# First transfers in pieces on two queues, first weights rounded in halves, two jobs' products in another order, half the warming products

## The chip, the cores and the metric

The kernel runs on one core of a Trainium2 chip. The metric is the device time of one execution in microseconds (us). Three runs of the kernel before took 1553.55, 1553.56 and 1553.8 us, so the median is 1553.56 us. The engines are called by their names in the profile: PE (TensorE, with PEld for its weight loads), DVE (VectorE), ACT (ScalarE), POOL (GpSimd) and SP (SyncE, which only issues transfers here).

## The reference, cut to what matters

Two transformer-like blocks run one behind the other on 512 tokens with 1024 features. The first has a gated recurrence, sparse attention chosen by an indexer, and a feed-forward part; the second has linear attention, window attention, cross attention and a convolutional feed-forward part. The change touches only the first microseconds, where the input is normed and the first columns of the first projection are made:

```python
def hybrid_layer(x, norm1_w, w_in, ...):
    h = rms_norm(x, norm1_w)
    u = h @ w_in
    rnn_x, rnn_gate, q, k, v, iq, ik, iw, g = jnp.split(u, offsets, axis=-1)
    ik = rms_norm(ik, idx_k_norm_w)
    y_attn = dsa_attention(q, k, v, iq, ik, iw)
    ...
```

All operands are fp32.

## The kernel before

**Jobs.** Activations lie with features on the 128 partitions and tokens along the row: `x` is 8 tiles of 128x512. A job makes 128 output features: its weights are one slot of `w_raw`, 128x1024, which are 8 blocks of 128x128, one for each input tile. There are four slots. Every factor is cut into a high part (rounded to fp32r) and a rest: ACT writes `w_hi` from `w_raw`, POOL writes `w_lo = w_raw - w_hi` in four pieces of 128x256, ACT writes `a_hi = x * norm1`, and DVE writes `a_lo`, the rest of that product. PE adds three products for each of the 8 tiles: `w_hi a_hi`, `w_hi a_lo` and `w_lo a_hi`, thus 24 products of 128x512 a job. The division by the root mean square of a token is made later, on the job's output, so that the jobs can start before the norm is known.

**The start.** Job 0 (J_IK: the indexer's keys and weights) and job 1 (J_IQ, the first tile of its queries) are written out by hand, product by product, so that PE can use whatever is ready: `whole` issues `w_hi a_hi`, `input_rest` issues `w_hi a_lo`, `weight_rest` issues `w_lo a_hi`. Everything is issued in order on each engine and waits on semaphores: `xhi_ready` counts the tiles of `a_hi`, `xlo_ready` those of `a_lo`, `hi_ready` the finished slots of `w_hi`, `lo_ready` the pieces of `w_lo`. Ahead of them PE multiplies zeros (the warming products, L696) since its clock starts low. From job 2 on `job` issues the three products of a tile in turn (L634 to L636).

**Transfers.** SP's queue is q1 in the profile, ACT's is q10. Before the change ACT issues `vec` (all 326 columns of the norms' and biases' values, 163 KB), four transfers of two tiles of `x` each (512 KB), and `cst` (276 KB). SP issues the weights of job 0 at once, and those of jobs 1 to 3 (512 KB each) each behind the landing of the next transfer of `x`. Weights from job 4 on wait for POOL to free their slot.

**Squares.** Behind `a_hi`, ACT squares the tiles of `x` and DVE adds them into `acc`; PE sums `acc` over the partitions behind job 2 (`norm_sum`), ACT takes the root, DVE the inverse, and PE spreads it within job 3.

Of the kernel before, what the change touches and what calls it, by code (L numbers as in the profile page):

```python
# [29 lines left out]
ACT = mybir.ActivationFunctionType  # L30
# [3 lines left out]
P = 128  # L34
T = 512
# [5 lines left out]
SLOTS = 4  # L41
# [3 lines left out]
J_IK = 0  # L45
J_IQ = 1
# [131 lines left out]
NVEC = 0  # L178
# [48 lines left out]
def build(nc, w_all, x_t, mem_t, vecs, consts, rg_w, consts2, row_table, out):  # L227
    with ExitStack() as ctx:
# [7 lines left out]
        raw = sb("w_raw", [P, SLOTS, KT * P])  # L236
        w_hi = sb("w_hi", [P, SLOTS, KT * P], F32R)
# [5 lines left out]
        vec = sb("vec", [P, NVEC])  # L243
        cst = sb("cst", [P, 4 * P + 40])
# [194 lines left out]

        @block.sync  # L440
        def _(sp):
            for sl in range(SLOTS):
                if sl >= 1:
                    sp.wait_ge(x_landed[sl], 16)
                sp.dma_start(raw[:, sl], w_all[sl]).then_inc(raw_landed[sl], 16)
            with sp.Fori(1, J_IN2 // SLOTS) as i:
                for sl in range(SLOTS):
# [176 lines left out]
        def _(pe):  # L624
# [67 lines left out]
                block_of(k, range(5, 8), hi, lo, width, 7, early(k, 0)).then_inc(s("job_done"), 1)  # L692

            pe.wait_ge(s("zeros_ready"), 1)
            for _ in range(5):
                mm(o_ps[:], p1[:, 0, 0:P], p1[:, 0, :], start=True, stop=True)  # L696

            def whole(k, kts):

                for kt in kts:  # L700
                    if k == J_IK:
                        pe.wait_ge(s("xhi_ready"), kt + 1)
                    if kt == 0:
# [24 lines left out]
            weight_rest(J_IK, (0, 1))
            whole(J_IK, (2, 3))
            weight_rest(J_IK, (2, 3))  # L730
            input_rest(J_IK, (1,))
            whole(J_IK, (4, 5))
            weight_rest(J_IK, (4, 5))
            input_rest(J_IK, (2,))
            whole(J_IK, (6, 7))
            weight_rest(J_IK, (6, 7))
            input_rest(J_IK, (3, 4))
            whole(J_IQ, (0, 1))
            input_rest(J_IK, (5,))
            whole(J_IQ, (2, 3, 4))  # L740
            weight_rest(J_IQ, (0, 1))
            input_rest(J_IK, (6,))
            whole(J_IQ, (5, 6, 7))
            weight_rest(J_IQ, (2, 3))
            input_rest(J_IK, (7,)).then_inc(s("job_done"), 1)
            input_rest(J_IQ, range(4))
            weight_rest(J_IQ, (4, 5))
            input_rest(J_IQ, range(4, 8))
            weight_rest(J_IQ, (6, 7)).then_inc(s("job_done"), 1)
            job(J_IQ + 1, a_hi, a_lo)  # L750
            pe.wait_ge(s("const_landed"), 16)
            norm_sum(0)
            norm_job(1, J_IQ + 2, a_hi, a_lo)
            pe.wait_ge(s("qk_sq"), 1)
# [775 lines left out]
        def _(act):  # L1530
# [42 lines left out]
            def load_x():
                for c in range(4):
                    act.dma_start(x[:, 2 * c:2 * c + 2, :],
                                  x_t[2 * c:2 * c + 2].rearrange("k p t -> p k t")).then_inc(x_landed[c], 16)


            act.dma_start(vec[:], vecs).then_inc(s("vec_landed"), 16)
            load_x()  # L1580
            act.dma_start(cst[:], consts).then_inc(s("const_landed"), 16)
            act.wait_ge(s("vec_landed"), 16)

            fn(small[:, 0:8], vcol("lam", 0, 8), ACT.Abs).then_inc(s("setup_step"), 1)
            for f in range(8):
                act.wait_ge(x_landed[f // 2], 16)
                fn(a_hi[:, f, :], x[:, f, :], ACT.Copy, scale=vcol("norm1", f)).then_inc(s("xhi_ready"), 1)
                if f == 0:
                    split(0)
            for f in range(8):  # L1590
                if f in (0, 2, 6):
                    split((1, 2, 3)[(0, 2, 6).index(f)])
                square_tile(0, f, x[:, f, :])
            split(4)
            act.wait_ge(s("setup_step"), 1)
            fn(small[:, 0:8], small[:, 0:8], ACT.Exp, scale=-1.0).then_inc(s("setup_step"), 1)
            act.wait_ge(s("setup_step"), 2)
            fn(small[:, 0:8], small[:, 0:8], ACT.Ln, bias=1.0).then_inc(s("setup_step"), 1)
            act.wait_ge(s("const_landed"), 16)
            fn(eps_sq, eps64, ACT.Copy, scale=EPS).then_inc(s("setup_step"), 1)  # L1600
            norm_root(1)
            take_rstd(1)
# [183 lines left out]

            act.wait_ge(s("att_pv"), 8)
            act.wait_ge(s("att_out"), 8)
            load_x()
            for f in range(8):  # L1790
                if f >= 1:
                    split(J_G1 + 3 + f)
# [471 lines left out]
        def _(dve):  # L2264
# [54 lines left out]


            v.memset(p1[:, 0, :], 0.0).then_inc(s("zeros_ready"), 1)
            dve.wait_ge(s("vec_landed"), 16)
            for f in range(8):
                dve.wait_ge(x_landed[f // 2], 16)
                lo_part(0, f, "norm1", a_hi, a_lo)
            for f in range(8):
                add_square(0, f)
# [1 line left out]
            take(J_IK, p1[:, 0, :])  # L2329
            take(J_IQ, p1[:, 1, :])  # L2330
            take(J_IQ + 1, p1[:, 2, :])
            dve.wait_ge(s("const_landed"), 16)
            did(ts(small[:, 8:16], vcol("lam", 0, 8), -1.0, 0.0, ALU.mult, ALU.max))
            dve.wait_ge(s("setup_step"), 3)
            settle()
# [249 lines left out]
                tt(s_lo[:, 2:4, c], s34, s_hi[:, 2:4, c].bitcast(F32), ALU.subtract).then_inc(s("ff_part"), 1)  # L2585

            for f in range(8):
                dve.wait_ge(x_landed[f // 2], 32)
# [681 lines left out]
```

## Time and profile before

| | |
|---|---|
| median of three runs | 1553.56 us |
| profiled execution | 1553.76 us, of which the span of the trace is 1552.0 us |
| PE busy in the span | 1537.9 us (99%) |
| PE's first warming product | 1.46 us |
| PE's first product of job 0 | 7.83 us |
| PE's first product of job 2 | 20.13 us |

The 1.76 us between the execution's time and its span lie before the first and behind the last instruction of the trace. Times in the rows below are us from the span's start. PE's products are pipelined: a row gives 0.39 us for one of 128x512, but the next starts 0.23 us later. A warming product is fp32 and appears as two passes, so that five of them are ten rows.

### The profile page before, as it was taken

The page shows a single profiled execution, that of the slowest core. Times are in us where ns is not written, and L with a number is a line of the kernel's source. Part 1 is how long each engine was busy: PE and PEld are TensorE (multiplying, and loading weights), DVE is VectorE, ACT ScalarE, POOL GpSimd, SP SyncE. Part 2 cuts the span into 40 slices and gives each one's busy share as a digit, 9 for nine tenths or more (in the row PEclk, how much of TensorE's full clock was granted, in tenths as well). Part 3 has the DMA queues.
Part 4 walks back from the last instruction along what each step waited for, and adds up shares of the span by engine and source line. Part 5 has one row for each costly group of instructions (what it writes and reads, how often), then busy time and mean ns, then how long its engine had stood idle before and what let it go on. Part 6 is the DMA issues. An engine that isn't in the chain of part 4 may idle for free. (4 is left out here: it accounts for less than half of the span.)

```text
span 1552.0 us, 23343 instructions
## 1 busy us (share of the span) xinstructions
PE 1537.9 (99%) x8238; PEld 1271.8 (82%) x8238; DVE 982.9 (63%) x1795; ACT 788.0 (51%) x1399; POOL 902.7 (58%) x904
## 2 busy tenths in 40 slices
PE   9999999999999999999999999999999999999998
PEld 6687776777888888888887887778988889999986
DVE  5496986665235776677766445763233887878864
ACT  6435786544325544444444434643654556565643
POOL 6344663323554677777765542256544488888854
PEclk9999999999999999999999999999999999999999
DMA  5322222123322233322333321133322223333331
GB/s 201 99 96 68 82 94 70 55 68 102 102 95 95 91 100 109 109 95 96 109 109 109 123 83 54 55 110 109 121 92 99 82 96 109 96 109 99 107 109 69
DMA packets 46168, 150.37 MB, mean 97 GB/s; under 512 B 4648, under 2 KB 9904, under 8 KB 46064
## 3 DMA queue, kind: packets, MB, share of 16 engines
q1 hardware_dynamic: 39648, 140.00, 27.3%
q10 hardware_dynamic: 6416, 8.98, 1.7%
q8 instruction: 65, 1.06, 0.3%
q14 instruction: 39, 0.32, 0.1%
HBM read 146.73 MB, written 2.11 MB: 96 GB/s over the span
## 5 line engine op out<-in xcount | busy, mean ns | idle before, releaser
L528 POOL TENSOR_TENSOR w_lo<-w_raw,w_hi 128x256 fp32r<-128x256 f32 x560 | 432.3, 804 | 452.7 <-ACT w_hi L1543 452.5
L534 POOL TENSOR_TENSOR w_lo<-w_raw,w_hi 128x512 fp32r<-128x512 f32 x218 | 295.3, 1370 | 171.7 <-ACT w_hi L1816 171.3
L634 PE MATMUL job<-a_hi,w_hi 128*128 128x512 f32 (+1 forms) x586 | 226.0, 386 | 0.0
L636 PE MATMUL job<-a_hi,w_lo 128*128 128x512 f32 (+1 forms) x586 | 221.4, 378 | 0.0
L635 PE MATMUL job<-a_lo,w_hi 128*128 128x512 f32 (+1 forms) x586 | 221.4, 378 | 0.0
L1543 ACT ACTIVATE w_hi<-w_raw 128x1024 fp32r<-128x1024 f32 x140 | 146.3, 1051 | 130.1 <-PE job L636 117.7
L1816 ACT ACTIVATE w_hi<-w_raw 128x512 fp32r<-128x512 f32 x218 | 133.5, 626 | 135.8 <-PE job L960 61.0
L2273 DVE TENSOR_TENSOR w_lo<-arena,w_hi 128x512 fp32r<-128x512 f32 x120 | 137.7, 1156 | 3.8 <-ACT w_hi L1816 3.2
L634 PEld LDWEIGHTS job<-a_hi,w_hi 128*128 128x128 f32 x586 | 110.2, 188 | 36.3 <-issue 13.2
L979 PE MATMUL score<-s_two,w_lo 128*128 128x256 f32 x480 | 135.3, 282 | 0.0
L634 PE MATMUL job<-b_two,w_hi 128*128 128x512 f32 x328 | 131.6, 401 | 1.8 <-DVE b_two L2270 1.2
L636 PE MATMUL job<-b_two,w_lo 128*128 128x512 f32 x328 | 128.0, 390 | 0.0
L635 PE MATMUL job<-b_two,w_hi 128*128 128x512 f32 x328 | 127.7, 389 | 0.0
L636 PEld LDWEIGHTS job<-a_hi,w_lo 128*128 128x128 f32 x586 | 110.2, 188 | 20.7
L635 PEld LDWEIGHTS job<-a_lo,w_hi 128*128 128x128 f32 x586 | 110.3, 188 | 19.1
L2273 DVE TENSOR_TENSOR arena<-arena,job 128x512 f32<-128x512 f32 (+1 forms) x108 | 73.2, 678 | 79.9 <-PE job L636 46.2
L960 PE MATMUL job<-a_hi,w_lo 128*128 128x512 f32 x300 | 116.7, 389 | 0.0
L959 PE MATMUL job<-a_lo,w_hi 128*128 128x512 f32 x300 | 116.7, 389 | 0.0
L958 PE MATMUL job<-a_hi,w_hi 128*128 128x512 f32 x300 | 116.7, 389 | 0.0
L1816 ACT ACTIVATE w_hi<-arena 128x512 fp32r<-128x512 f32 x120 | 75.2, 628 | 61.3 <-PE job L960 28.9
L2273 DVE TENSOR_TENSOR arena<-job,rstd 128x512 f32<-128x512 f32 x66 | 45.3, 687 | 94.0 <-PE job L636 80.6
L979 PE MATMUL score<-b_two,w_lo 128*128 128x256 f32 x360 | 101.5, 282 | 0.0
(453 smaller groups left out, 3639.1 us busy)
## 6 DMA issues: line engine op xcount, KB each, us to landing
w_raw<-w_all SPq DMA_DIRECT2D x264, 512.0 KB, 3.2
arena<-x_t ACTq DMA_DIRECT2D x8, 512.0 KB, 6.2
out_t<-arena SPq DMA_DIRECT2D x6, 256.0 KB, 2.1
arena<-rg_w ACTq DMA_DIRECT2D x1, 1024.0 KB, 5.9
arena<-mem_t ACTq DMA_DIRECT2D x1, 1024.0 KB, 6.8
spare<-row_table ACTq DMA_DIRECT2D x3, 256.0 KB, 3.8
arena<-consts ACTq DMA_DIRECT2D x1, 512.0 KB, 3.6
out_t<-arena ACTq DMA_DIRECT2D x2, 256.0 KB, 2.5
```

The source lines that it names most:

```text
L528: nc.gpsimd.tensor_tensor(w_lo[:, sl, c], raw[:, sl, c], w_hi[:, sl, c].bitcast(F32), ALU.subtract).then_inc(s("lo_ready"), 1)
L534: nc.gpsimd.tensor_tensor(ff_tile(w_lo, tag), ff_source(tag), ff_tile(w_hi, tag).bitcast(F32), ALU.subtract).then_inc(s("ff_raw_low"), 1)
L634: mm(ps[:, 0:n], w_hi[:, sl, c], hi[:, kt, 0:n], start=kt == 0, stop=False)
L635: mm(ps[:, 0:n], w_hi[:, sl, c], lo[:, kt, 0:n], start=False, stop=False)
L636: ins = mm(ps[:, 0:n], w_lo[:, sl, c], hi[:, kt, 0:n], start=False, stop=kt == last)
L958: mm(ps[:], wh[:, w], hi[:, h0 + kt, :], start=kt == first, stop=False)
L959: mm(ps[:], wh[:, w], lo[:, h0 + kt, :], start=False, stop=False)
L960: ins = mm(ps[:], wl[:, w], hi[:, h0 + kt, :], start=False, stop=kt == last)
L979: ins = mm(ps[:, 0:256], wl[:, c], x2[:, 0], start=False, stop=kt == 3, skip_group_check=True)
L1543: fn(w_hi[:, sl], raw[:, sl], ACT.Copy).then_inc(s("hi_ready"), 1)
L1816: fn(ff_tile(w_hi, tag), ff_source(tag), ACT.Copy).then_inc(s("ff_high"), 1)
L2273: return v.tensor_tensor(out_, a, b, op)
```

## The change

1. **Transfers.** `vec` is cut in its first 8 columns (`norm1`, 4 KB) and the other 318 (159 KB). `x` goes in parts of 1, 2, 2 and 3 tiles (`X_PARTS`); the third part (tiles 3 and 4) goes on SP's queue, the others on ACT's. The weights of job 0 go as two halves (256 KB each) at the head of SP's queue. SP then waits for the second part of `x` (tiles 1 and 2), and issues the weights of job 1, the rest of `vec`, `cst`, and the weights of jobs 2 and 3 without a further wait.
2. **First weights.** ACT rounds the first half of job 0's weights ahead of the first tile of `x`, and the second half behind the second tile. `hi_ready`, on which POOL waits, is set by the second half. PE's first four whole products of job 0 wait only for `a_hi`, which ACT makes behind the first half.
3. **ACT's first instruction** (the absolute value of `lam`) moves behind the squares and the rounding of job 4.
4. **Products.** The products of job 0 stand in another order, and job 1's all stand behind job 0's. Each job has the same 24 products as before.
5. **Warming.** Five products of 128x512 become two of 128x512 and one of 128x256.
6. A later load of `x`, near 378 us, goes in the parts of 1, 2, 2 and 3 tiles too, all on ACT's queue.

```diff
+X_PARTS = ((0, 1), (1, 3), (3, 5), (5, 8))
+X_PART = [c for c, (first, end) in enumerate(X_PARTS) for _ in range(first, end)]
+N_FIRST = 8
...
         def _(sp):
-            for sl in range(SLOTS):
-                if sl >= 1:
-                    sp.wait_ge(x_landed[sl], 16)
+            sp.dma_start(raw[:, 0, 0:T], w_all[0, :, 0:T]).then_inc(s("first_landed"), 16)
+            sp.dma_start(raw[:, 0, T:2 * T], w_all[0, :, T:2 * T]).then_inc(raw_landed[0], 16)
+            sp.dma_start(x[:, 3:5, :], x_t[3:5].rearrange("k p t -> p k t")).then_inc(x_landed[2], 16)
+            sp.wait_ge(x_landed[1], 16)
+            sp.dma_start(raw[:, 1], w_all[1]).then_inc(raw_landed[1], 16)
+            sp.dma_start(vec[:, N_FIRST:NVEC], vecs[:, N_FIRST:NVEC]).then_inc(s("const_landed"), 16)
+            sp.dma_start(cst[:], consts).then_inc(s("const_landed"), 16)
+            for sl in range(2, SLOTS):
                 sp.dma_start(raw[:, sl], w_all[sl]).then_inc(raw_landed[sl], 16)
...
-            for _ in range(5):
-                mm(o_ps[:], p1[:, 0, 0:P], p1[:, 0, :], start=True, stop=True)
+            for n in (T, T, 256):
+                mm(o_ps[:, 0:n], p1[:, 0, 0:P], p1[:, 0, 0:n], start=True, stop=True)
...
-                    if kt == 0:
+                    if kt == (4 if k == J_IK else 0):
                         pe.wait_ge(s("hi_ready"), k + 1)
...
-            act.dma_start(vec[:], vecs).then_inc(s("vec_landed"), 16)
-            load_x()
-            act.dma_start(cst[:], consts).then_inc(s("const_landed"), 16)
-            act.wait_ge(s("vec_landed"), 16)
-
-            fn(small[:, 0:8], vcol("lam", 0, 8), ACT.Abs).then_inc(s("setup_step"), 1)
+            act.dma_start(vec[:, 0:N_FIRST], vecs[:, 0:N_FIRST]).then_inc(s("first_landed"), 16)
+            load_x((0, 1, 3))
+            act.wait_ge(s("first_landed"), 32)
+            fn(w_hi[:, 0, 0:T], raw[:, 0, 0:T], ACT.Copy)
             for f in range(8):
-                act.wait_ge(x_landed[f // 2], 16)
+                act.wait_ge(x_landed[X_PART[f]], 16)
                 fn(a_hi[:, f, :], x[:, f, :], ACT.Copy, scale=vcol("norm1", f)).then_inc(s("xhi_ready"), 1)
-                if f == 0:
-                    split(0)
+                if f == 1:
+                    act.wait_ge(raw_landed[0], 16)
+                    fn(w_hi[:, 0, T:2 * T], raw[:, 0, T:2 * T], ACT.Copy).then_inc(s("hi_ready"), 1)
...
```

ACT at the program's start, before. `arena` holds `x`; the waits stand in brackets.

```order
L1579 DMA vec<-vecs 128x326
L1575 DMA arena<-x_t 128x2x512 x4
L1581 DMA cst<-consts 128x552
L1584 ACT_TABLE_LOAD
L1584 ACTIVATE small<-vec 128x8 [waits vec_landed]
L1587 ACTIVATE a_hi<-arena,vec 128x512 [waits x_landed0]
L1543 ACTIVATE w_hi<-w_raw 128x1024 [waits raw_landed0]
L1587 ACTIVATE a_hi<-arena,vec 128x512 [waits x_landed0]
L1587 ACTIVATE a_hi<-arena,vec 128x512 [waits x_landed1] x2
```

The same place of ACT now.

```order
L1586 DMA vec<-vecs 128x8
L1583 DMA arena<-x_t 128x512
L1583 DMA arena<-x_t 128x2x512
L1583 DMA arena<-x_t 128x3x512
L1589 ACT_TABLE_LOAD
L1589 ACTIVATE w_hi<-w_raw 128x512 [waits first_landed]
L1592 ACTIVATE a_hi<-arena,vec 128x512 [waits x_landed0]
L1592 ACTIVATE a_hi<-arena,vec 128x512 [waits x_landed1]
L1595 ACTIVATE w_hi<-w_raw 128x512 [waits raw_landed0]
L1592 ACTIVATE a_hi<-arena,vec 128x512 [waits x_landed1]
L1592 ACTIVATE a_hi<-arena,vec 128x512 [waits x_landed2] x2
```

Tile 1 of `a_hi` now waits for the second part of `x`, where it waited for the first, and the row that sets `hi_ready` stands behind it.

PE at the end of job 0 and in job 1, before. `job` is the accumulator.

```order
L721 MATMUL job<-a_lo,w_hi 128x512 [waits xlo_ready] x2
L705 MATMUL job<-a_hi,w_hi 128x512 [waits hi_ready]
L705 MATMUL job<-a_hi,w_hi 128x512
L721 MATMUL job<-a_lo,w_hi 128x512 [waits xlo_ready]
L705 MATMUL job<-a_hi,w_hi 128x512 x3
L712 MATMUL job<-a_hi,w_lo 128x512 [waits lo_ready]
L712 MATMUL job<-a_hi,w_lo 128x512
L721 MATMUL job<-a_lo,w_hi 128x512 [waits xlo_ready]
L705 MATMUL job<-a_hi,w_hi 128x512 x3
L712 MATMUL job<-a_hi,w_lo 128x512 [waits lo_ready]
L712 MATMUL job<-a_hi,w_lo 128x512
L721 MATMUL job<-a_lo,w_hi 128x512 [waits xlo_ready]
```

The same place of PE now.

```order
L713 MATMUL job<-a_hi,w_hi 128x512 [waits xhi_ready]
L720 MATMUL job<-a_hi,w_lo 128x512 [waits lo_ready]
L720 MATMUL job<-a_hi,w_lo 128x512
L729 MATMUL job<-a_lo,w_hi 128x512 [waits xlo_ready] x2
L713 MATMUL job<-a_hi,w_hi 128x512 [waits hi_ready]
L713 MATMUL job<-a_hi,w_hi 128x512 x7
L729 MATMUL job<-a_lo,w_hi 128x512 x4
L720 MATMUL job<-a_hi,w_lo 128x512 [waits lo_ready]
L720 MATMUL job<-a_hi,w_lo 128x512
```

Before, 12 products of job 1 (8 of `w_hi a_hi` and 4 of `w_lo a_hi`) stood ahead of job 0's last `a_lo` product; now none does.

## Rows read from the trace of the kernel before

**Rows 1.** The page: the span and PE's busy time.

```profile
span 1552.0 us, 23343 instructions
PE 1537.9 (99%) x8238; PEld 1271.8 (82%) x8238; DVE 982.9 (63%) x1795; ACT 788.0 (51%) x1399; POOL 902.7 (58%) x904
```

**Rows 2.** Waits of PE, whole span: total us, times, longest.

```profile
PE job L705 <- ACT w_hi L1543: 0.4, 1, 0.4
```

**Rows 3.** Timeline of PE, 0 to 26 us: start, us, what.

```profile
1.46 6.50 PE L696 MATMUL o<-arena 128*128 128x512 f32 x10 [1.46 <-DVE arena L2321]
7.83 0.47 PE L705 MATMUL job<-a_hi,w_hi 128*128 128x512 f32 x1
...
20.13 0.39 PE L634 MATMUL score<-a_hi,w_hi 128*128 128x512 f32 x1
20.36 0.39 PE L635 MATMUL score<-a_lo,w_hi 128*128 128x512 f32 x1
...
25.57 0.95 PE L664 MATMUL o<-cst,acc 128*128 128x2 f32 x8
```

**Rows 4.** Timeline of PE's weight loads, within the warming products.

```profile
4.18 0.34 PEld L696 LDWEIGHTS o<-arena 128*128 128x128 f32 x1 [0.52 <-issue]
5.04 0.34 PEld L696 LDWEIGHTS o<-arena 128*128 128x128 f32 x1 [0.52 <-issue]
...
6.09 0.19 PEld L696 LDWEIGHTS o<-arena 128*128 128x128 f32 x1 [0.24 <-issue]
6.52 0.19 PEld L696 LDWEIGHTS o<-arena 128*128 128x128 f32 x1 [0.24 <-issue]
```

**Rows 5.** Timeline of ACT, 0 to 12 us.

```profile
1.20 2.16 ACTq L1575 DMA_DIRECT2D arena<-x_t  x4
3.39 0.58 ACTq L1581 DMA_DIRECT2D cst<-consts  x1
4.00 1.28 ACT L1584 ACT_TABLE_LOAD   x1 [4.00 <-issue]
...
6.01 0.72 ACT L1587 ACTIVATE a_hi<-arena,vec 128x512 fp32r<-128x512 f32 x1 [0.52 <-DMA arena<-x_t]
6.64 1.04 ACT L1543 ACTIVATE w_hi<-w_raw 128x1024 fp32r<-128x1024 f32 x1
7.59 4.39 ACT L1587 ACTIVATE a_hi<-arena,vec 128x512 fp32r<-128x512 f32 x7
```

**Rows 6.** Timeline of SP: the weights of jobs 1 and 2.

```profile
7.85 0.34 SPq L445 DMA_DIRECT2D w_raw<-w_all  x1
9.12 0.33 SPq L445 DMA_DIRECT2D w_raw<-w_all  x1
```

**Rows 7.** Transfers of 0 to 40 us, GB/s in each us.

```profile
GB/s 0 41 258 365 391 375 371 381 410 412 293 356 397 348 406 332 33 0 8 250 266 0 0 66 373 102 0 160 356 8 205 320 0 0 0 0 66 295 164 78
```

**Rows 8.** Queues in 2.5 to 3.5 us: packets, MB, share.

```profile
q1 hardware_dynamic: 66, 0.27, 71.1%
q10 hardware_dynamic: 65, 0.08, 23.3%
```

**Rows 9.** Timeline of DVE, 8 to 24 us.

```profile
8.40 1.33 DVE L2270 SCALAR_TENSOR_TENSOR a_lo<-arena,vec,a_hi 128x512 fp32r<-128x512 f32 x1 [0.77 <-ACT a_hi L1587]
...
11.96 0.74 DVE L2270 SCALAR_TENSOR_TENSOR a_lo<-arena,vec,a_hi 128x512 fp32r<-128x512 f32 x1
...
15.11 0.96 DVE L2305 COPY acc<-sq 128x512 f32<-128x512 f32 x1
16.18 7.93 DVE L2273 TENSOR_TENSOR acc<-acc,sq 128x512 f32<-128x512 f32 x7
```

**Rows 10.** Timeline of POOL, 7 to 29 us.

```profile
7.76 3.72 POOL L528 TENSOR_TENSOR w_lo<-w_raw,w_hi 128x256 fp32r<-128x256 f32 x4 [7.31 <-ACT w_hi L1543]
13.90 15.03 POOL L528 TENSOR_TENSOR w_lo<-w_raw,w_hi 128x256 fp32r<-128x256 f32 x16 [2.42 <-ACT w_hi L1543]
```

More of the change, by code:

```diff
@@ L727, in _ @@
             whole(J_IK, (1,))
+            input_rest(J_IK, (1,))
+            whole(J_IK, (2,))
             weight_rest(J_IK, (0, 1))
-            whole(J_IK, (2, 3))
+            whole(J_IK, (3,))
+            input_rest(J_IK, (2,))
+            whole(J_IK, (4,))
             weight_rest(J_IK, (2, 3))
-            input_rest(J_IK, (1,))
-            whole(J_IK, (4, 5))
+            input_rest(J_IK, (3,))
+            whole(J_IK, (5,))
             weight_rest(J_IK, (4, 5))
-            input_rest(J_IK, (2,))
-            whole(J_IK, (6, 7))
+            input_rest(J_IK, (4,))
+            whole(J_IK, (6,))
+            input_rest(J_IK, (5,))
+            whole(J_IK, (7,))
             weight_rest(J_IK, (6, 7))
[L737 to L745, printed above, removed]
+            input_rest(J_IK, (6, 7)).then_inc(s("job_done"), 1)
+            whole(J_IQ, range(8))
             input_rest(J_IQ, range(4))
-            weight_rest(J_IQ, (4, 5))
+            weight_rest(J_IQ, range(4))
             input_rest(J_IQ, range(4, 8))
-            weight_rest(J_IQ, (6, 7)).then_inc(s("job_done"), 1)
+            weight_rest(J_IQ, range(4, 8)).then_inc(s("job_done"), 1)
             job(J_IQ + 1, a_hi, a_lo)
-            pe.wait_ge(s("const_landed"), 16)
+            pe.wait_ge(s("const_landed"), 32)
             norm_sum(0)
@@ L1571, in prep, with load_x @@
                     square_tile(n, f, x[:, f, :])
[L1573 to L1576, printed above, removed]
-            act.dma_start(vec[:], vecs).then_inc(s("vec_landed"), 16)
-            load_x()
-            act.dma_start(cst[:], consts).then_inc(s("const_landed"), 16)
-            act.wait_ge(s("vec_landed"), 16)
-            fn(small[:, 0:8], vcol("lam", 0, 8), ACT.Abs).then_inc(s("setup_step"), 1)
+            def load_x(parts):
+                for c in parts:
+                    r = slice(*X_PARTS[c])
+                    act.dma_start(x[:, r, :], x_t[r].rearrange("k p t -> p k t")).then_inc(x_landed[c], 16)
+            act.dma_start(vec[:, 0:N_FIRST], vecs[:, 0:N_FIRST]).then_inc(s("first_landed"), 16)
+            load_x((0, 1, 3))
+            act.wait_ge(s("first_landed"), 32)
+            fn(w_hi[:, 0, 0:T], raw[:, 0, 0:T], ACT.Copy)
             for f in range(8):
-                act.wait_ge(x_landed[f // 2], 16)
+                act.wait_ge(x_landed[X_PART[f]], 16)
                 fn(a_hi[:, f, :], x[:, f, :], ACT.Copy, scale=vcol("norm1", f)).then_inc(s("xhi_ready"), 1)
-                if f == 0:
-                    split(0)
+                if f == 1:
+                    act.wait_ge(raw_landed[0], 16)
+                    fn(w_hi[:, 0, T:2 * T], raw[:, 0, T:2 * T], ACT.Copy).then_inc(s("hi_ready"), 1)
             for f in range(8):
@@ L1594, in _ @@
             split(4)
+            act.wait_ge(s("const_landed"), 32)
+            fn(small[:, 0:8], vcol("lam", 0, 8), ACT.Abs).then_inc(s("setup_step"), 1)
             act.wait_ge(s("setup_step"), 1)
@@ L1598, in _ @@
             fn(small[:, 0:8], small[:, 0:8], ACT.Ln, bias=1.0).then_inc(s("setup_step"), 1)
-            act.wait_ge(s("const_landed"), 16)
             fn(eps_sq, eps64, ACT.Copy, scale=EPS).then_inc(s("setup_step"), 1)
@@ L1788, in _ @@
             act.wait_ge(s("att_out"), 8)
-            load_x()
+            load_x(range(4))
             for f in range(8):
@@ L2321, in _ @@
             v.memset(p1[:, 0, :], 0.0).then_inc(s("zeros_ready"), 1)
-            dve.wait_ge(s("vec_landed"), 16)
+            dve.wait_ge(s("first_landed"), 32)
             for f in range(8):
-                dve.wait_ge(x_landed[f // 2], 16)
+                dve.wait_ge(x_landed[X_PART[f]], 16)
                 lo_part(0, f, "norm1", a_hi, a_lo)
@@ L2331, in _ @@
             take(J_IQ + 1, p1[:, 2, :])
-            dve.wait_ge(s("const_landed"), 16)
+            dve.wait_ge(s("const_landed"), 32)
             did(ts(small[:, 8:16], vcol("lam", 0, 8), -1.0, 0.0, ALU.mult, ALU.max))
@@ L2587, in _ @@
             for f in range(8):
-                dve.wait_ge(x_landed[f // 2], 32)
+                dve.wait_ge(x_landed[X_PART[f]], 32)
                 add_to_x(J_OUT + f, f)
```

## The prediction

> **What bounds the kernel.** I read first the page's busy times: PE is busy for 1537.9 of 1552.0 us [rows 1], so the time is PE's work and what PE waits for. Then PE's waits: the one in the changed code is 0.4 us [rows 2]. So any gain or loss is where PE stands when the hand-written part ends, the first product of job 2 at 20.13 us [rows 3]. Behind it everything is released by PE's own products, directly or over ACT, DVE and POOL, except the norm's sum, checked below; I let a shift there reach the end one for one.
>
> Between PE's first product at 7.83 us and 20.13 us lie 12.30 us. A product starts 0.23 us behind the one ahead (20.13 to 20.36 [rows 3]); more exactly, job 2's 24 products take 20.13 to 25.57, that is 0.227 us each. The 48 products of jobs 0 and 1 need 10.9 us, so 1.4 us are waits spread among them. That, the first product's start, and any new wait are what the change can move. Without a single wait, and with the first product at 5.9 us (below), job 2 would start at 16.8, 3.3 us earlier: the ceiling of the gain, 0.2% of the time.
>
> **The transfers, which decide.** The 16 engines that move data are full from about 3 us on at 0.37 to 0.41 MB/us [rows 7], so order is all that matters. While both queues had work they took turns packet by packet: 66 packets of q1 and 65 of q10 in one us [rows 8]. Packets were 4 KB for weights and 1.3 KB for `vec` (0.27 MB in 66, 0.08 in 65), so the weights had three quarters of the bytes. Now all the large ones are rows of 2 KB (a half slot of weights, a tile of `x`), and the two queues get half each.
>
> Before, tiles 0 and 1 of `x` landed together at 6.01 [rows 5], and tiles 2 and 3 at 7.85, where SP's wait on them ended [rows 6]. Up to the latter, 0.17 MB of `vec`, 0.52 of weights and four tiles of 0.26 had to move: 1.74 MB.
> - *Tile 0 now.* q10 has 8 columns of `vec` and one tile ahead, q1 has the two halves. The tile needs some 0.26 MB on each queue beside `vec`'s packets, 0.55 to 0.6 MB; rows 7 add up to 0.66 MB by 4.0 us. With the 0.6 to 1 us that landings lag behind this sum (1.22 MB had to move for the landing at 6.01, and the sum reaches that at 5.4) it lands at 4.6 to 5.2; I take 5.1.
> - *Tiles 1 and 2 now.* q10 needs `vec`'s first columns and three tiles, 0.79 MB; in the same turns q1 moves its 1.05 MB (both halves, tiles 3 and 4): 32 packets an engine on either queue (8+8+16 and 16+16). So 1.84 MB have moved when tiles 1 and 2 are complete, 0.10 MB more than the 1.74 before. At 0.38 MB/us that is 0.27 us behind 7.85: 8.1 us. Bounds: if q10 were served with only the first weight half ahead, 1.05 MB, 6.0 us (the landing at 6.01 had 1.22 MB); if each packet costs by number, 8.6. I take 8.1, since rows 8 show the turns.
> - *Tiles 5 to 7* follow alone: 0.79 MB more, 2.63 MB, which rows 7 reach at about 9.1; with the same lag 10.1 us, not late, since ACT is there at about 11.
>
> **ACT.** It issues three transfers of `x` instead of four and no `cst`: 2.16/4 = 0.54 us and 0.58 us less [rows 5], so the table load ends at 4.2 instead of 5.3. The first half of the weights is rounded then (0.63 us, half of 1.04 with the fixed part), hidden in the wait for tile 0. Tile 0's `a_hi` runs 5.1 to 5.8, 0.9 us earlier than before. But tile 1, which was at 7.59, waits for 8.1. Then come `a_hi` 1 (to 8.8), the second half (0.53 us behind), and the others at 4.39/7 = 0.61 us: `a_hi` 2 is done at 9.95, `a_hi` 7 at 13.0. `hi_ready` comes at 9.4 where it came at 7.7, so POOL starts its rests at 9.4 instead of 7.76 [rows 10].
>
> **DVE, the chain that PE follows.** An `a_lo` costs 0.74 us when POOL is idle (11.96) and 1.2 to 1.33 us, a step of 1.15, while POOL works (8.40) [rows 9, 10]. Tile 0's is done at 6.7. Tile 1's runs 8.9 to 9.6. Tile 2's starts at 10.0 beside POOL, and 3 and 4 follow in steps of 1.15 to 13.5. POOL's four pieces last 9.4 to about 13.6; it starts job 1's at 14.0, when ACT has rounded them. So tile 5 is cheap (done 14.2) and 6 and 7 are dear: `a_lo` 7 ends at 16.5. Before, it ended at 15.19 (the copy at 15.11 begins at its end).
>
> **PE.** It finishes job 0 only behind `a_lo` 7: 16.55 + 0.23 = 16.8. Its other products of job 0 were possible earlier (POOL's last piece 13.6, `a_hi` 7 13.0), so nothing else is late. Then all 24 products of job 1 follow, 24 x 0.227 = 5.45: job 2 starts at 22.2. Before, 12 of them filled the wait for `a_lo`; now PE stands still in these gaps. Sum: 22.2 - 20.13 = +2.1 us. Broken down: +1.3 us from the later `a_lo` 7, and +0.8 us since its last use is now followed by 5.7 us of products, where before the products at 15.19 still to come were 4.9 us (15.19 to 20.13).
>
> **The rest of the change.**
> - *Warming*: five products of 2 passes lasted to 7.8 us; the first four passes took 0.86 us each (4.18 to 5.04), later ones 0.43 (6.09 to 6.52) [rows 4]: the clock rose from 1.2 to 2.4 GHz near 5.4 us. The new ones end at about 5.6. This costs nothing by itself, because the first product waits for `a_hi` until 5.85; the price of a fallen clock is a rival below.
> - *`lam`'s absolute value*, 0.2 us on ACT, stands now ahead of the norm's root, where ACT has 0.5 us to spare: 0.
> - *The norm*: `acc` was complete at 24.11 (16.18 + 7.93 [rows 9]) and PE asks at 25.57 [rows 3]. Now DVE starts 1.4 us later, 25.5, and PE asks at 27.7: 0.
> - *Weights of jobs 1 to 3*: the same bytes are ahead of job 3's as before. Job 1's are issued at 8.1 (7.85 before) and pass `vec` and `cst`; ACT wants them at 12.9. 0, or 0.3 us either way.
> - *The second load of `x`* near 378 us: no engine waited for it before; 0.
>
> Against the profiled execution, 1553.76 + 2.1 = 1555.9; it lies 0.2 us over the median, so 1555.7 for the median.
>
> **Rivals.**
> 1. *ACT's queue gets more than half* and tiles 1 and 2 land near 6.0 us. For it: SP's third transfer is issued only near 1.5 us, and a queue can start late. Against it: rows 8. Then `hi_ready` is at 7.2, tiles 3 and 4 come in time, `a_lo` 7 ends at 13.7 to 14.4 and job 2 starts at 19.4 to 20.1: 0 to -0.7 us, 1552.9 to 1553.6. The point from which it decides is 6.0 to 6.3 us; each 0.1 us later costs 0.1.
> 2. *The clock falls back.* PE has two products between 5.65 and 8.9, then three in each 1.15 us. In the warming stretch the rise came 3.9 us behind the first product (1.46 to 5.4, [rows 3, 4]). If the clock is at 1.2 GHz when job 1 begins and comes back as late, 9 products at 0.43 instead of 0.227 are +1.9 us, together +4: 1557.7. A fall that ends before 16 us is hidden in PE's gaps. The Trainium skill ("TensorE: Matmul & The Clock Gate", Part 1) says that the low clock is the default and that an idle array returns to it; by that rule the halved warming and the gap could cost this. The trace shows the rise, but no fall.
> 3. *Tiles 1 and 2 land at 8.6 or later*, since 128 packets of 32 bytes and twice the packets of weights cost by number: +2.6 to +3.5, 1556.5.
>
> **Chances.** Forecast 65% (its own range 1554.9 to 1556.5), rival 1 15%, rival 2 11%, rival 3 9%. My range is 1552.9 to 1557.8. 0.2% is 3.1 us, about what can be told from no change: faster by over that would need the ceiling above, 3%. Slower by over it, from 1556.7, is rival 2, part of rival 3 and the forecast's edge, 18%. Within, 79%.
>
> **What would show it.** Right: `a_hi` 0 near 5.1 us, a gap on ACT until about 8.1 that ends with a transfer of `x`, POOL's first piece near 9.4, PE's gaps released by DVE's `a_lo`, `a_lo` 7 ending near 16.5, the first L642 product near 22.2. Wrong: tile 1 landing before 7 us, or `a_lo` 7 ending before 15, or PE's products behind 17 us at 0.43 us.

## The result and the profile after

The changed kernel takes 1557.1 us in the median of 19 runs (1556.51 to 1558.36), the kernel before 1553.78 us in as many (1553.29 to 1554.52). The ratio is 1.0022, with a 95% interval of 1.0015 to 1.0028: 3.3 us slower. The forecast was 1555.7 us, with the range 1552.9 to 1557.8. The measured time lies in that range, but outside the forecast's own one (1554.9 to 1556.5). The direction and the path were as forecast; the loss was 1.2 us larger than the 2.1 us forecast.

The profiled execution took 1557.0 us, its span is 1555.2 us. PE's timeline of the changed kernel, as in [rows 3]: start, us, what.

```profile
1.46 4.46 PE L704 MATMUL o<-arena 128*128 128x512 f32 x6 [1.46 <-DVE arena L2328]
6.05 0.49 PE L713 MATMUL job<-a_hi,w_hi 128*128 128x512 f32 x1
6.95 0.50 PE L729 MATMUL job<-a_lo,w_hi 128*128 128x512 f32 x1 [0.40 <-DVE a_lo L2277]
9.63 0.79 PE L713 MATMUL job<-a_hi,w_hi 128*128 128x512 f32 x1 [2.17 <-ACT a_hi L1592]
10.48 0.80 PE L729 MATMUL job<-a_lo,w_hi 128*128 128x512 f32 x1
...
17.43 0.62 PE L729 MATMUL job<-a_lo,w_hi 128*128 128x512 f32 x2
17.88 1.98 PE L713 MATMUL job<-a_hi,w_hi 128*128 128x512 f32 x8
...
23.32 0.39 PE L642 MATMUL score<-a_hi,w_hi 128*128 128x512 f32 x1
```

The first product starts 1.8 us earlier than before, and job 2 starts 3.2 us later: at 23.32 instead of 20.13 [rows 3]. Between the second and the third product PE waits 2.17 us for ACT's second tile. What ACT did then, as in [rows 5]:

```profile
2.70 1.28 ACT L1589 ACT_TABLE_LOAD   x1 [2.70 <-issue]
4.11 0.63 ACT L1589 ACTIVATE w_hi<-w_raw 128x512 fp32r<-128x512 f32 x1
5.28 0.72 ACT L1592 ACTIVATE a_hi<-arena,vec 128x512 fp32r<-128x512 f32 x1 [0.54 <-DMA arena<-x_t]
8.85 0.72 ACT L1592 ACTIVATE a_hi<-arena,vec 128x512 fp32r<-128x512 f32 x1 [2.85 <-DMA arena<-x_t]
9.48 0.61 ACT L1595 ACTIVATE w_hi<-w_raw 128x512 fp32r<-128x512 f32 x1
10.00 3.77 ACT L1592 ACTIVATE a_hi<-arena,vec 128x512 fp32r<-128x512 f32 x6
```

ACT itself waits 2.85 us for a transfer of `x`: tiles 1 and 2 land at 8.85, and the second half of job 0's weights is rounded only behind the first of them. The queues' rows for 3 to 7 us (packets, MB, share) show that the two share the engines as the prediction had it:

```profile
q1 hardware_dynamic: 336, 0.64, 47.0%
q10 hardware_dynamic: 333, 0.63, 42.2%
```

DVE and POOL start accordingly. DVE's timeline, as in [rows 9]:

```profile
9.68 0.75 DVE L2277 SCALAR_TENSOR_TENSOR a_lo<-arena,vec,a_hi 128x512 fp32r<-128x512 f32 x1 [2.78 <-ACT a_hi L1592]
10.81 6.47 DVE L2277 SCALAR_TENSOR_TENSOR a_lo<-arena,vec,a_hi 128x512 fp32r<-128x512 f32 x6 [0.38 <-ACT a_hi L1592]
17.21 0.96 DVE L2312 COPY acc<-sq 128x512 f32<-128x512 f32 x1
```

POOL's, as in [rows 10]:

```profile
10.17 4.27 POOL L536 TENSOR_TENSOR w_lo<-w_raw,w_hi 128x256 fp32r<-128x256 f32 x4 [9.72 <-ACT w_hi L1595]
14.80 15.53 POOL L536 TENSOR_TENSOR w_lo<-w_raw,w_hi 128x256 fp32r<-128x256 f32 x16 [0.36 <-ACT w_hi L1550]
```

DVE's last `a_lo` ends at 17.28 (10.81 + 6.47) instead of 15.19. The change of order gives this end another weight. In the kernel before, the product that uses it is the first of these five:

```profile
17.19 1.29 PE L721 MATMUL job<-a_lo,w_hi 128*128 128x512 f32 x5
```

That is 2.0 us behind its end, so PE did not wait for it. In the changed kernel it is used near 17.65 (the second product of the row at 17.43), 0.4 us behind its end, and all of job 1 still has to follow.

The windows of the changed kernel show one thing more. Columns: stretch, its length, busy time and number of instructions of PE, PEld, DVE, ACT and POOL, the granted clock, the share and the GB/s of the transfers.

```profile
8.00:9.00 1.00, 0.00 (x0) 0.00 (x0) 0.00 (x0) 0.15 (x1) 0.00 (x0) 1.00 1.05 406
9.00:10.00 1.00, 0.37 (x1) 0.28 (x1) 0.32 (x1) 1.00 (x2) 0.00 (x0) 0.51 0.85 277
10.00:12.00 2.00, 1.94 (x5) 1.29 (x5) 1.62 (x3) 2.00 (x5) 1.83 (x2) 0.50 0.96 303
12.00:14.00 2.00, 2.00 (x6) 1.58 (x5) 2.00 (x3) 2.00 (x4) 2.00 (x3) 0.50 0.74 239
14.00:16.00 2.00, 2.00 (x6) 1.55 (x5) 2.00 (x2) 1.76 (x3) 1.64 (x3) 0.54 0.94 378
16.00:18.00 2.00, 2.00 (x10) 1.62 (x10) 2.00 (x3) 1.06 (x1) 2.00 (x3) 1.00 0.87 334
```

Behind the gap in PE's work the granted clock is 0.50, that is 1.2 GHz, from about 9 to nearly 16 us. "PE busy 2.00" hides this: six products fill 2 us there, ten do so at 1.00. From 11.08 us on PE's products follow each other without a wait, first 0.43 us and then 0.23 us apart, so that PE's own products, and not a wait for DVE, set the time at which `a_lo` 7 is used in this execution; run 1 below shows that it would be about 0.2 us earlier without the low clock.

The record has the mean granted clock of every execution. In five of the 19 it was 0.995, and they took 1557.36 to 1558.36 us (median 1558.15); the other 14, the profiled one among them, had 0.996 to 0.998 and a median of 1556.98. In a quarter of the executions the clock was thus low for longer, and they took 1.2 us more. None of the five was profiled, so that it is not shown where in them it was low: it can be at the start, or in the last microseconds of the program, where run 6 below loses 0.9 us.

The shift is then carried to the end undiminished. The chain that ended last, of the changed kernel:

```profile
1542.21 1.05 PE o L1525 x8
1543.26 0.59 PE o L1509 x4
```

The same two steps of the kernel before:

```profile
1538.99 1.05 PE o L1518 x8
1540.05 0.59 PE o L1502 x4
```

They start 3.22 and 3.21 us earlier; job 2 was 3.19 us earlier.

### The profile page after: what moved, and what is told of

Its sections match the earlier page's. It is cut to its first block and busy times, and to the rows that moved or that the text cites. A ratio compares the mean times of both kernels' runs of the same rounds, so it can differ in the third digit from the quotient of the medians.

```text
span 1555.2 us, 23338 instructions
## 1 busy us (share of the span) xinstructions
PE 1538.9 (99%) x8234; PEld 1273.2 (82%) x8234; DVE 979.9 (63%) x1795; ACT 788.3 (51%) x1400; POOL 904.4 (58%) x904
```

## The experiments

Each was timed 11 times. The runs fall in three series (1 to 4, 5 to 8 and 9 to 12), in each of which the kernel before was timed 33 times, with medians of 1554.05, 1554.03 and 1553.7 us; "to before" is the difference from the median of the same series. Where the interval holds 1.0, the difference can't be told from none by it: this is so in runs 5 to 10 and 12, and run 4 stands at the edge. "Job 2" is the start of its first product in that run's profiled execution, the measure that tells most here, since the whole loss is made ahead of it. It is one execution of each, and not always a typical one: that of run 1 was the shortest of its 11 (1556.02 us), that of run 6 took 0.7 us more than its median.

| run | median us | to before | ratio, 95% interval | `a_hi` 1 us | `a_lo` 7 ends | job 2 |
|---|---|---|---|---|---|---|
| before | 1553.78 | | | 7.59 | 15.19 | 20.13 |
| changed | 1557.1 | +3.3 | 1.0015 to 1.0028 | 8.85 | 17.28 | 23.32 |
| 1 changed, 5 warming products | 1557.16 | +3.1 | 1.0011 to 1.0029 | 8.59 | 16.57 | 22.42 |
| 2 changed, old order | 1557.3 | +3.3 | 1.0014 to 1.0032 | 8.90 | 17.33 | 23.62 |
| 3 changed, both | 1556.78 | +2.7 | 1.0006 to 1.0024 | 9.14 | 17.57 | 23.52 |
| 4 changed, tiles 3, 4 on ACT's queue | 1555.12 | +1.1 | 1.0 to 1.0018 | 7.55 | 15.51 | 21.37 |
| 5 runs 3 and 4 together | 1554.29 | +0.3 | 0.9994 to 1.0012 | 7.70 | 15.69 | 20.55 |
| 6 before, new order | 1554.9 | +0.9 | 0.9998 to 1.0016 | 7.60 | 15.18 | 21.04 |
| 7 before, half the warming | 1554.3 | +0.3 | 0.9994 to 1.0012 | 7.69 | 15.16 | 20.60 |
| 8 before, `vec` cut at 8 | 1554.55 | +0.5 | 0.9995 to 1.0013 | 7.37 | 14.45 | 20.57 |
| 9 before, weights in halves | 1554.21 | +0.5 | 0.9993 to 1.0011 | 8.12 | 15.68 | 20.64 |
| 10 before, `vec` cut at 128 | 1554.19 | +0.5 | 0.9995 to 1.0013 | 7.51 | 15.12 | 20.06 |
| 11 changed, `vec` whole | 1556.52 | +2.8 | 1.0008 to 1.0026 | 8.64 | 16.59 | 22.45 |
| 12 the best guess | 1554.17 | +0.5 | 0.9995 to 1.0013 | 7.62 | 15.59 | 20.50 |

`a_hi` 1 is the start of ACT's second tile. The theory of the prediction (L) is that the landing of tiles 1 and 2 sets DVE's chain and that PE follows it. The rivals are that the low clock costs the time (C), and, once the transfers had been seen to be slower than before at 4 to 8 us, that this slow stretch has a cause of its own (D).

**1. Five warming products in the changed kernel.**

```diff
-            for n in (T, T, 256):
+            for n in (T, T, T, T, T):
```

> The changed kernel with the five warming products of before. Theory L (the landing of tiles 1 and 2 of x sets DVE's a_lo chain, and PE follows it; the low clock is hidden in PE's waits): a_lo 7 still ends near 17.3 us, job 2 still starts at 23.0 to 23.3 us, the time is 0 to 0.3 us below the changed kernel. Theory C (the low clock from 9 to 16 us is what costs): with the longer warming the clock stays high, job 2 starts before 22 us and the time falls by over 1 us.

The time does not move (1557.16). Job 2 started 0.9 us earlier in the profile, but 0.7 of that is DVE's chain: 0.26 us from the landing, and 0.45 us since POOL paused 0.7 us behind its first four pieces and DVE was quicker meanwhile. PE's timeline of this run: the warming now reaches to near 9 us by its modelled end, so that the gap is short, and the products behind it run at the high clock.

```profile
1.46 7.49 PE L704 MATMUL o<-arena 128*128 128x512 f32 x10 [1.46 <-DVE arena L2328]
...
16.62 0.50 PE L729 MATMUL job<-a_lo,w_hi 128*128 128x512 f32 x1 [0.39 <-DVE a_lo L2277]
```

The second row is the last product of job 0: here PE waits for `a_lo` 7, which ended at 16.57, as theory L says.

What C can claim is what remains: from the end of `a_lo` 7 to job 2 it is 5.85 us here and 6.04 us in the changed kernel, 0.2 us. The 11 executions say the same without the profile: their mean granted clock was 0.998 or 0.999 in each, as in the kernel before, where the changed kernel has 0.995 to 0.998, and their median is still 3.1 us above the kernel before.

**2 and 3. The product order of before in the changed kernel; then with five warming products as well.** The hand-written order of jobs 0 and 1 is put back word for word.

> The changed kernel with the product order of before in jobs 0 and 1. Theory L with a low clock: PE can now work on job 1 while it waits for a_lo, but at 0.43 us a product it has little to spare: 48 products, some 16 of them at 0.43 between 9 and 16 us, then 0.227 each, job 2 at 22.6 to 23.0, 0.3 to 0.7 us below the changed kernel. If the order is worth what the prediction said (0.8 us) whatever the clock: 22.5. If the order is worth nothing: 23.3.

> The changed kernel with both the product order and the five warming products of before; only the transfers, the halves and lam's place are changed. Theory L: a_lo 7 ends near 17.3 us. If five warming products keep the clock high, 13 products remain behind a_lo 7, 3.0 us, job 2 at 20.5 to 20.9, 2.5 us below the changed kernel. If the clock falls all the same in PE's gap near 9 us, as in e2: 22.6 to 23.0.

Both expectations were too good: 23.62 and 23.52. PE, in the order of before, is no longer held by DVE. Two other things hold it. The old order asks for a product with `w_lo` right behind the second whole product, and POOL starts `w_lo` only when the second half of the weights is rounded (at 10.22 and 10.46 in these runs, at 7.76 before). Run 2:

```profile
11.12 1.22 PE L720 MATMUL job<-a_hi,w_lo 128*128 128x512 f32 x2 [0.65 <-POOL w_lo L536]
```

In run 3 this wait is 0.94 us. Then PE has the rest of its 48 products to do, and these run partly at the low clock: in run 3 the clock was granted at 0.63 and 0.52 in 12 to 14 and 14 to 16 us, and tiles 1 and 2 had landed only at 9.14. Run 3's times spread from 1555.0 to 1558.09, the widest of these runs, and they follow the clock: the three executions with a mean of 0.999 took 1555.0, 1555.05 and 1555.87 us, the seven with 0.998 have a median of 1556.86, and the one with 0.997 took 1558.09. So behind such a gap the order brought nothing measurable alone, and with the warming 0.4 us in the median (less than the intervals can tell) and more only where the clock stayed up.

**4. Tiles 3 and 4 of `x` behind tiles 1 and 2 on ACT's queue.** SP's queue then holds only the two weight halves.

```diff
-            sp.dma_start(x[:, 3:5, :], x_t[3:5].rearrange("k p t -> p k t")).then_inc(x_landed[2], 16)
...
-            load_x((0, 1, 3))
+            load_x((0, 1, 2, 3))
```

> The changed kernel with tiles 3 and 4 of x on ACT's queue behind tiles 1 and 2, so that SP's queue holds only the two weight halves. Theory L (turns between the queues): tiles 1 and 2 land when 1.31 MB have moved and not 1.84, near 7.4 us instead of 8.85; a_lo 7 ends near 15.8, job 2 starts near 21.8, 1.5 us below the changed kernel. Rival D (the slow stretch of the transfers at 4 to 6 us comes from the many small pieces, whichever queue): tiles 1 and 2 land at 8.2 or later, under 0.7 us gained.

Measured: tiles 1 and 2 at 7.55 instead of 8.85, `a_lo` 7 at 15.51 instead of 17.28, job 2 at 21.37, 1.95 us earlier, and the time 2.2 us nearer to the kernel before (+1.1 instead of +3.3). All 11 executions (1555.04 to 1556.06 us) lie below all 19 of the changed kernel (from 1556.51 us). The timeline of this run, ACT at the second tile:

```profile
7.55 0.72 ACT L1591 ACTIVATE a_hi<-arena,vec 128x512 fp32r<-128x512 f32 x1 [0.96 <-DMA arena<-x_t]
```

DVE's `a_lo` 2 to 7:

```profile
9.51 6.00 DVE L2276 SCALAR_TENSOR_TENSOR a_lo<-arena,vec,a_hi 128x512 fp32r<-128x512 f32 x6 [0.38 <-ACT a_hi L1591]
```

PE at job 2:

```profile
21.37 0.39 PE L641 MATMUL score<-a_hi,w_hi 128*128 128x512 f32 x1
```

One transfer moved from one queue to the other gives back two thirds of the loss. This is the run that shows theory L.

**5. Runs 3 and 4 together.**

> The changed kernel with tiles 3 and 4 of x on ACT's queue, the product order of before and five warming products. Theory L: tiles 1 and 2 land near 7.5 us and a_lo 7 ends near 15.5, as with tiles 3 and 4 moved alone. PE then has 46 products from about 8.3 us on, 10.4 us, and some 1 us of waits: job 2 at 19.5 to 20.0 if the clock stays high, near the kernel before or up to 0.6 us below it (1553.5 to 1554.1). If the clock falls, which the lone products before 8.3 us may cause, 3.4 us at half speed add up to 1.7 us: 1555.5.

1554.29 us, +0.3: it can't be told from the kernel before. Job 2 at 20.55 was later than expected; here the clock rose late, and the warming held PE's first product back to 8.46 us:

```profile
8.46 0.79 PE L712 MATMUL job<-a_hi,w_hi 128*128 128x512 f32 x1
```

**6. Only the new order, in the kernel before.** The new hand-written order replaces the old one; nothing else is changed.

> The kernel before with only the new order of products in jobs 0 and 1 (transfers, halves and warming as before). Theory L: a_lo 7 ends at 15.2 us as before, but 24 products of job 1 and the last of job 0 come behind it, 5.8 us: job 2 at 21.0 instead of 20.13, +0.9 us. If PE's gaps let the clock fall as well: +1.5 or more. If the order is worth nothing: +0.2 at most.

DVE's chain is untouched and job 2 starts 0.91 us later. The median is 0.9 us higher, which its interval alone does not tell from none; the profile does, since the shift is still 0.92 us at the product that stands at 1538.99 in the kernel before and at 1539.91 here. From the timeline of this run, DVE:

```profile
15.10 0.95 DVE L2304 COPY acc<-sq 128x512 f32<-128x512 f32 x1
```

PE:

```profile
21.04 0.39 PE L634 MATMUL score<-a_hi,w_hi 128*128 128x512 f32 x1
```

The first row (DVE) shows the copy that follows `a_lo` 7, at 15.10 as against 15.11 before; the second (PE) is job 2. With the new order job 2 comes 5.85 or 5.86 us behind the end of `a_lo` 7 (runs 1, 4, 6 and 11), and PE follows DVE. With the old order this distance is not fixed (4.86 to 6.29 us over the runs). What is nearly fixed there, where the clock is high, is the time from PE's first product of job 0 to job 2: 12.30 us in the kernel before and 12.09, 12.10, 12.28 and 12.04 in runs 5, 8, 9 and 10. In the kernel before PE is held by its own 48 products and a few short waits.

The profiled execution took 1.8 us more than that of the kernel before, twice the shift of job 2. The other 0.9 us are made in the last 4 us of the program, where PE waits 1.07 and 0.56 us and then has eight small products left. PE's last row, in the kernel before and in run 6, and the window of run 6 around it, whose granted clock is 0.50:

```profile
1546.11 0.61 PE L1510 MATMUL score<-cst,rcol 128*128 128x128 f32 x4
...
1547.50 1.06 PE L1509 MATMUL score<-cst,rcol 128*128 128x128 f32 x4
...
1547.00:1548.00 1.00, 1.00 (x7) 1.00 (x6) 0.46 (x2) 0.00 (x0) 0.00 (x0) 0.50 0.70 247
```

In the kernel before the granted clock is 1.00 until 1548 us, behind the last product. The profiles of runs 9 and 10, with other edits, have such a fall too, with some 0.4 us in each, and most of the others have none. So it goes by the execution, it seems, and not by the order of jobs 0 and 1; no kernel was profiled twice to show that.

**7. Only half the warming, in the kernel before.**

```diff
-            for _ in range(5):
-                mm(o_ps[:], p1[:, 0, 0:P], p1[:, 0, :], start=True, stop=True)
+            for n in (T, T, 256):
+                mm(o_ps[:, 0:n], p1[:, 0, 0:P], p1[:, 0, 0:n], start=True, stop=True)
```

> The kernel before with only the warming products cut to half. Theory L: the first product of job 0 waits for w_hi until 7.8 us in any case and PE is dense from there on, so 0 to +0.2 us. Theory C (the halved warming is what costs): the clock is low in some part of 8 to 14 us and job 2 starts 1 us later or more.

Between the two theories: job 2 is 0.47 us later; the median is 0.3 us higher, not to be told from none. PE waits 2.1 us ahead of its first product, and then the clock is low for a while:

```profile
9.00:10.00 1.00, 1.00 (x4) 0.79 (x3) 1.00 (x2) 1.00 (x3) 1.00 (x2) 0.50 1.05 410
10.00:12.00 2.00, 2.00 (x6) 1.53 (x5) 2.00 (x3) 2.00 (x4) 2.00 (x2) 0.50 1.04 415
12.00:14.00 2.00, 2.00 (x9) 1.63 (x9) 2.00 (x4) 1.59 (x4) 0.51 (x2) 0.96 1.02 418
```

Some seven products at 0.43 instead of 0.23 us would be 1.5 us by estimate; that only 0.47 us are left is put down to the old order's 1.4 us of waits, which the slower products fill.

**8 and 10. Only `vec` cut, in the kernel before**, at 8 columns and at 128, with `lam`'s absolute value moved as in the change; a small activation is left in its old place.

```diff
-            act.dma_start(vec[:], vecs).then_inc(s("vec_landed"), 16)
+            act.dma_start(vec[:, 0:8], vecs[:, 0:8]).then_inc(s("vec_landed"), 16)
             load_x()
+            act.dma_start(vec[:, 8:NVEC], vecs[:, 8:NVEC]).then_inc(s("const_landed"), 16)
```

> The kernel before with only vec cut: its first 8 columns ahead, the other 318 behind x, and the absolute value of lam moved as in the change (a small activation keeps the table load early). By bytes alone 0.16 MB less are ahead of x: tiles 0 and 1 land near 5.6 us and tiles 2 and 3 near 7.4 instead of 6.0 and 7.85; job 2 starts 0 to 0.4 us earlier. Rival D (the packets of 32 bytes bring the slow stretch of the transfers at 4 to 5.5 us): the stretch shows, and nothing lands earlier, 0 to +0.4 us.

> The kernel before with vec cut as in the run that sends 8 columns ahead, but with 128 columns (512 bytes a packet) ahead and 198 behind. Theory D (packets of 32 bytes bring the slow stretch): no slow stretch, 0.1 MB less ahead of x, tiles 2 and 3 land near 7.6 us, job 2 at 19.9 to 20.1. Rival (it comes from one more transfer on ACT's queue, whatever its size): the stretch shows as with 8 columns, tiles 2 and 3 land at 8.2 or later and job 2 starts at 20.4 or later.

Neither gained time (both +0.5, not to be told from none). In run 8 the second tile came 0.2 us and `a_lo` 7 0.7 us earlier than before, and job 2 was still 0.4 us later: the warming lasted longer, PE's first product came at 8.47 instead of 7.83, and PE does not wait for `a_lo` 7 in this order. Run 10's job 2 is at 20.06, as before.

**9. Only the first weights transferred in halves, in the kernel before.**

```diff
+            sp.dma_start(raw[:, 0, 0:T], w_all[0, :, 0:T]).then_inc(s("vec_landed"), 16)
+            sp.dma_start(raw[:, 0, T:2 * T], w_all[0, :, T:2 * T]).then_inc(raw_landed[0], 16)
```

> The kernel before with only job 0's weights transferred as two halves (rounded as a whole, as before). Theory T (the turns between queues): the packets of weights are 2 KB now, so that x gets half of the bytes against the weights instead of a third; the same bytes are ahead of tiles 2 and 3, which land at 7.8 to 8.0 us; no slow stretch at 4 to 6 us; job 2 at 20.1 to 20.3. Rival S (the slow stretch comes from the pieces of weights): it shows here, tiles 2 and 3 land at 8.3 or later, job 2 at 20.4 or later.

**11. The changed kernel with `vec` whole.**

```diff
-            act.dma_start(vec[:, 0:N_FIRST], vecs[:, 0:N_FIRST]).then_inc(s("first_landed"), 16)
+            act.dma_start(vec[:], vecs).then_inc(s("first_landed"), 16)
```

> The changed kernel with vec whole and first, as before (0.16 MB more ahead of tiles 1 and 2, no packets of 32 bytes). Theory D: no slow stretch, 2.0 MB land by about 8.4 to 8.6 us, 0.3 us earlier than with the cut; job 2 near 22.9, 0 to 0.5 us below the changed kernel. Rival: the stretch stays, tiles 1 and 2 land at 9.2, the time rises by 0.4 us.

These four are about the transfers. The window of 4 to 8 us of run 8, the last number in GB/s:

```profile
4.00:8.00 4.00, 4.00 (x6) 1.52 (x5) 0.75 (x1) 3.62 (x5) 0.45 (x1) 1.00 0.95 314
```

The same of run 9:

```profile
4.00:8.00 4.00, 4.00 (x7) 1.68 (x6) 0.59 (x1) 2.95 (x4) 0.00 (x0) 1.00 1.05 383
```

In the same window the kernel before has 379, run 6 has 359, run 7 has 372 and run 11 has 361: with run 9, all with `vec` whole are at 359 to 383. The changed kernel has 331, runs 1 to 5, 10 and 12 have 329, 341, 319, 333, 330, 336 and 304: all with `vec` cut are at 304 to 341, whether at 8 columns or at 128. So D is half right. The cut goes with slower transfers right behind it, by some 0.045 MB/us, 0.18 MB over 4 us, which is about the 0.16 MB that it takes out of the way. In the changed kernel the bytes are missing in 4 to 6 us, and the engines that move the data stood idle there for a part of the time. The window of 4 to 5 us, in the kernel before, in the changed kernel and in run 11 (the share of the transfers is the last number but one):

```profile
4.00:5.00 1.00, 1.00 (x2) 0.34 (x1) 0.00 (x0) 1.00 (x1) 0.00 (x0) 1.00 1.02 391
4.00:5.00 1.00, 1.00 (x2) 0.34 (x1) 0.00 (x0) 0.63 (x1) 0.00 (x0) 1.00 0.71 227
4.00:5.00 1.00, 1.00 (x2) 0.33 (x1) 0.00 (x0) 0.38 (x1) 0.00 (x0) 1.00 1.05 391
```

But it is not the 32 bytes of a packet, since 512 bytes (runs 10, 12) did not mend it, and not the halves of the weights (run 9). Why it is so stays open. In time it is little: run 11, which undoes the cut, is 0.5 us better against its kernel before than the changed kernel, and in its profile tiles 1 and 2 land 0.2 us earlier, with 0.16 MB more ahead of them. Run 9's halves land tile 0 later (its `a_hi` starts at 6.54 instead of 6.01, that of the second tile at 8.12 instead of 7.59), as the two queues now moved 190 and 215 packets, 0.33 and 0.35 MB, in 3 to 5 us; its first product, its `a_lo` 7 and its job 2 were each 0.5 us later.

**12. The best guess**: `vec` cut at 128 columns, tiles 3 and 4 on ACT's queue, halves rounded as in the change, old order, five warming products.

> What the runs point to as the best of the changed kernel: vec cut at 128 columns, tiles 3 and 4 of x on ACT's queue, halves rounded as in the change, product order of before, five warming products. Theories L and D: tiles 1 and 2 land near 7.2 us, 46 products from 7.9 us with 1 us of waits, job 2 at 19.4 to 19.9, 0.3 to 0.6 us below the kernel before, 1553.4 to 1553.8. Rival: the warming products end at 8.4 us, as once when the clock rose late, or the stretch stays: no better than the kernel before.

1554.17 us, +0.5. No version here beats the kernel before. PE's first product was at 7.32 and yet job 2 started at 20.50. The second tile of `x` came at 7.62, about when it did before (7.59 for its `a_hi`), and behind it PE waited for POOL's first piece of `w_lo`:

```profile
8.94 4.28 POOL L535 TENSOR_TENSOR w_lo<-w_raw,w_hi 128x256 fp32r<-128x256 f32 x4 [8.49 <-ACT w_hi L1595]
...
9.84 0.73 PE L719 MATMUL job<-a_hi,w_lo 128*128 128x512 f32 x2 [0.94 <-POOL w_lo L535]
```

In the kernel before POOL starts at 7.76 [rows 10] and PE has no such wait. The rounding in halves, with the second half behind the second tile, brings the first half forward and holds POOL back. No run takes this part of the change out by itself, so its price with the old order is not measured beyond this wait.

## Why the prediction held, and what was too small

- *The range*: the forecast's own range ended at 1556.5, and 1557.1 lies outside it. The stated range reached to 1557.8 only through rival 2, whose course (a clock still low when job 1 begins) is not what the profiled execution shows. That the measured time lies inside is in part luck; the sizes that came are those of rival 3, which had 9%.
- *Where the time is decided*: right. The whole loss is made before job 2 (3.19 us there, 3.2 at the end).
- *Tile 0 and ACT's early start*: right (5.28 against 5.1), and worthless, as forecast: the first product was 1.8 us earlier and gained nothing.
- *Tiles 1 and 2*: the mechanism was right, the size not. This is the term that was mis-sized: "At 0.38 MB/us that is 0.27 us behind 7.85: 8.1 us". They landed at 8.85. The bytes were counted well (the two queues moved 0.64 and 0.63 MB in 3 to 7 us), but the rate was taken from the kernel before. What failed is the premise that the engines "are full from about 3 us on": their share was 0.71 and 0.88 in 4 to 5 and 5 to 6 us, and they moved 227 and 307 GB/s where it was 391 and 375 before. These 0.23 MB are by estimate 0.6 of the missing 0.75 us at 0.38 MB/us; the rest stays open. Run 4 shows the mechanism, and runs 8 to 11 that the lower rate goes with the cut of `vec`. Rival 3 had the size (8.6 or later, +2.6 to +3.5 us); of its reason, that packets cost by number, the part on the weights' packets is refuted by run 9 and the 32 bytes by runs 10 and 12.
- *DVE's chain behind it*: right. From tile 1's start on ACT to the end of `a_lo` 7 the forecast had 8.4 us; it was 8.43. It is 7.95 to 8.0 us in the runs where POOL pauses 0.6 to 0.8 us behind its first four pieces (1, 4, 5, 11 and 12), so that landing and chain are not quite independent.
- *The new order*: right for the kernel before. The forecast had +0.8 us from it; run 6 shows 0.91 by itself. In the changed kernel the old order gives nothing back (run 2: 1557.3 us), since there it meets POOL's late start and the low clock, so that the 0.91 us are not what one would win by taking this part of the change out.
- *The clock*: rival 2's fall happened, and cost little. It was low until nearly 16 us, and the prediction had a fall that ends before 16 us as hidden in PE's gaps; 0.2 us were not hidden in the profiled execution (6.04 against 5.85). In the five of 19 with a mean clock of 0.995 a low clock goes with 1.2 us more. If it lay at the start, PE, which has no wait left behind 11 us, would be held by its own products, as rival 2 had it; but it can lie at the program's end as well, and no profile shows one of them. The rule of the Trainium skill ("TensorE: Matmul & The Clock Gate", Part 1), that an idle array returns to the low clock, held here and in run 7 (0.50 granted behind waits of 2.17 and 2.14 us). With the old order the same low clock costs more, since PE then has fewer gaps to hide it in (runs 2, 3).
- *The rest*: `norm_sum`, `lam` and the later load of `x` cost nothing, since the shift at the end equals that at job 2.

The sum by the profiles, in the prediction's own terms: `a_lo` 7 ends 2.09 us later (forecast 1.3), and from there to job 2 it is 6.04 instead of 4.94 us, 1.10 more (forecast 0.8), of which 0.91 is the order by run 6 and 0.19 the clock; together 3.19 us.

## What to carry to other kernels

Two queues that are busy together share the engines packet by packet (336 and 333 packets in 3 to 7 us here), so a transfer put on a free queue is paid for by the transfer that the next engine waits for: order by need over both queues taken together, and count the bytes of both. An earlier first product is worth nothing if the second has to wait; what counts is the last link of the chain that PE follows, and how many products are left behind it. Filling PE's waits with work of the next job is worth its time (0.9 us in the kernel before), but only while that work's own inputs are there: with POOL's rests late and the clock low, it brought nothing. A gap in PE's work can cost the clock as well. And where one execution is profiled, compare its time with the median before its rows are taken as typical.

## What was not expected of the hardware

- With `vec` cut in two transfers, 304 to 341 GB/s were moved in 4 to 8 us in nine profiles; with `vec` whole 359 to 383 in five. In the changed kernel a part of it is idle time of the engines that move the data (share 0.71 in 4 to 5 us against 1.02). The cause is open.
- The same five warming products, which start at 1.46 us in every run, lasted 6.42 us in run 12 and 7.56 us in run 5. A pass takes 0.43 us less at the high clock [rows 4], so the 1.14 us between them are, by estimate, a clock that rose some 2.3 us later. The clock column of the windows doesn't show this: it has 1.00 from 2 us on, while the passes still take 0.86 us. Warming by a count of products is not a fixed time, and it delayed PE's first product (7.32 against 8.46 us). PE's timeline of run 12:

```profile
1.46 6.42 PE L703 MATMUL o<-arena 128*128 128x512 f32 x10 [1.46 <-DVE arena L2328]
7.32 0.79 PE L712 MATMUL job<-a_hi,w_hi 128*128 128x512 f32 x1
```

That of run 5:

```profile
1.46 7.56 PE L703 MATMUL o<-arena 128*128 128x512 f32 x10 [1.46 <-DVE arena L2328]
```

- The clock can fall in the last waits of the program too, as the profile of run 6 shows: its last eight products took 0.9 us more than those of the kernel before. A difference of some tenths of a us between two profiled executions can come from there alone, so the rows up to 1540 us are the better measure of a change at the start.
